# Prompt attention on one Trainium2 core: value tiles stationary, two query tiles moving

## What is computed

```python
# fox: causal, with a forgetting bias
s = q @ k.T * SCALE + (q_cum - k_cum);   p = softmax(where(k_pos <= q_pos, s));   o = p @ v
# nsa, selected branch (here all 16 blocks of 64 keys are selected, so it is causal over all keys)
s = q @ k_sel.T * SCALE + rel_bias;      p = softmax(causal);                      o_s = p @ v_sel
# nsa, window branch: the last 512 keys
s = q @ k_win.T * SCALE + rel_bias;      p = softmax(0 <= dist < 512);             o_w = p @ v_win
o = gate_c * o_c + gate_s * o_s + gate_w * o_w
```

## Time and profile before

| | |
|---|---|
| median of 3 runs | 2388.65 us (2384.7 to 2396.48) |
| profiled execution | 2383.58 us, its span 2381.8 us |
| busy: PE, PEld, DVE, ACT, POOL | 85%, 74%, 41%, 32%, 18% of the span |
| stage of `prompt_attention` | 874 to 1321 us |
| mean granted clock of TensorE | 0.91 of 2.4 GHz over the span, 0.97 in the stage |

### The profile page before, as it was taken

The page is one execution under the profiler, slowest core; times in us unless marked ns, Lnnn a source line. Parts: engine busy times, 40 slices in busy tenths (PEclk is TensorE's granted clock), DMA queues, the critical chain, the costliest instruction groups (busy, mean ns, idle before and its releaser), DMA issues. The chain is left out here.

```text
span 2381.8 us, 35846 instructions
## 1 busy us (share of the span) xinstructions
PE 2024.5 (85%) x12308; PEld 1761.7 (74%) x12308; DVE 979.1 (41%) x2016; ACT 771.3 (32%) x1469; POOL 431.5 (18%) x566
## 2 busy tenths in 40 slices
PE   3995979995637489999999488599999999799997
PEld 3884977785324489888988366599999999676764
DVE  2334223013223257676767521433333333355554
ACT  3223011112112126565656410322222222244454
POOL 4310002145061321121111000021212122000000
PEclk9896989997878559999999699699999999899998
DMA  5523635327683922232300041311111111402001
GB/s 128 96 66 105 206 143 185 116 72 196 217 266 125 169 62 54 54 79 55 68 16 1 31 140 69 110 44 45 44 44 53 35 53 35 150 32 71 26 27 47
DMA packets 164114, 210.37 MB, mean 88 GB/s; under 512 B 43420, under 2 KB 119509, under 8 KB 163863
## 3 DMA queue, kind: packets, MB, share of 16 engines
q1 hardware_dynamic: 136250, 125.09, 18.2%
q0 software_dynamic: 27744, 83.78, 12.6%
HBM read 173.84 MB, written 40.18 MB: 90 GB/s over the span
## 5 line engine op out<-in xcount | busy, mean ns | idle before, releaser
L118 PE MATMUL y_acc<-w_down_split_hi,act_split_hi 128*128 128x512 f32 (+1 forms) x396 | 164.6, 416 | 19.9 <-DVE act_split_lo L2623 17.9
L118 PE MATMUL gate_acc<-h_T_hi,w_gate_split_hi 128*128 128x352 f32 x528 | 172.6, 327 | 9.0 <-POOL w_gate_split_lo L2473 9.0
L120 PE MATMUL gate_acc<-h_T_hi,w_gate_split_lo 128*128 128x352 f32 x528 | 170.9, 324 | 0.0
L119 PE MATMUL gate_acc<-h_T_lo,w_gate_split_hi 128*128 128x352 f32 x528 | 170.6, 323 | 0.0
L118 PE MATMUL up_acc<-h_T_hi,w_up_split_hi 128*128 128x352 f32 x528 | 170.2, 322 | 0.0
L120 PE MATMUL up_acc<-h_T_hi,w_up_split_lo 128*128 128x352 f32 x528 | 169.3, 321 | 0.0
L119 PE MATMUL up_acc<-h_T_lo,w_up_split_hi 128*128 128x352 f32 x528 | 169.3, 321 | 0.0
L2171 ACT ACTIVATE pa_scores<-pa_scores,pa_neg_max 128x128 f32<-128x128 f32 (+1 forms) x192 | 144.1, 751 | 68.9 <-DVE pa_neg_max L2205 62.3
L2179 ACT ACTIVATE pa_probs_T_hi<-pa_t 128x512 fp32r<-128x512 f32 (+3 forms) x288 | 125.0, 469 | 106.6 <-PE pa_t L2133 105.2
L2234 DVE TENSOR_TENSOR pa_probs_T_lo<-pa_t,pa_probs_T_hi 128x512 fp32r<-128x512 f32 (+3 forms) x288 | 144.7, 530 | 32.8 <-ACT pa_probs_T_hi L2179 30.8
L119 PE MATMUL y_acc<-w_down_split_lo,act_split_hi 128*128 128x512 f32 (+1 forms) x396 | 157.5, 398 | 0.0
(11 more groups left out here) (409 smaller groups left out, 4939.0 us busy)
## 6 DMA issues: line engine op xcount, KB each, us to landing
fox_k_pages<-in_cache_fox_kv SPq DMA_DIRECT2D x64, 256.0 KB, 8.7
w_rows<-in_cache_fox_kv POOLq DMA_DIRECT2D x64, 256.0 KB, 6.5
w_gate<-in_w_gu SPq DMA_DIRECT2D x22, 512.0 KB, 3.9
w_up<-in_w_gu SPq DMA_DIRECT2D x22, 512.0 KB, 3.9
w_down_half<-in_w_down SPq DMA_DIRECT2D x22, 512.0 KB, 3.9
sel_pages<-in_cache_nsa_kv POOLq DMA_DIRECT2D x64, 128.0 KB, 7.6
pa_k_fox<-scratch_kf_d POOLq DMA_DIRECT2D x32, 256.0 KB
w_rows<-in_w_in SPq DMA_DIRECT2D x3, 2048.0 KB, 14.4
```

The source lines that it names most:

```text
L118: pe.matmul(out, a[0][at], b[0][bt], start=start, stop=False)
L119: pe.matmul(out, a[0][at], b[1][bt], start=False, stop=False)
L120: return pe.matmul(out, a[1][at], b[0][bt], start=False, stop=stop)
```

## The change

Units are taken in pairs (query tiles 2p and 2p + 1; NPR = 24 pairs in a turn of the loop). The value tile, its hi and lo halves side by side (128 columns), is now stationary, and the turned probabilities of both query tiles (256 columns) move. The result O is transposed: 128 rows (64 of the hi values, 64 of the lo) by 2 x 128 queries. ScalarE copies it to SBUF (`oT`), and `back(p)` makes two plain float32 products of it with `add_halves` (two 64x64 identities stacked), which turn it back and add the two halves. VectorE copies that to the job's output. Where a key tile counts for only one of the two query tiles, the slot of the other holds zeros, which POOL writes once. Key tiles are laid out in `pT` by slots, counted from the last one down. Beside this, constants that only the sample attention uses go into a table of their own (`c_smisc`), some tiles move to other phases or shrink, the ninth value tile goes away, and a local name in `down` changes.

```diff
+    NPR = NU // 2
+    def slots(s):
+        j, t = units[s]
+        out = []
+        for key in range(t, first_tile(s) - 1, -1):
+            r = t // 2 * 2 + 1 - key
+            out.append((key, NT if jobs[j][1] == "win" and t % 2 == 0 and r == 5 else r))
+        return out
+    def pair_slots(p):
+        seen = dict((slot, key) for s in (2 * p, 2 * p + 1) for key, slot in slots(s))
+        return sorted(seen.items())
...
-        scaled = ph.sb("pa_job_scaled", [P, NT, HD])
-        pT = [split(ph, f"pa_probs_T{i}", [P, T]) for i in range(2)]
+        pT = [split(ph, f"pa_probs_T{i}", [P, NT + 1, 2, P]) for i in range(2)]
+        oT = [ph.sb(f"pa_out_T{i}", [P, 2 * P]) for i in range(2)]
...
+            for both in pT:
+                for t in both:
+                    for slot, half in ((0, 0), (NT, 1)):
+                        pool.tensor_copy(t[:, slot, half, :], c.zero[:, :].to_broadcast([P, P])).then_inc(s_z, 1)
...
-            pe.wait_ge(pa.s_vz, 6)
+            pe.wait_ge(s_z, 12)
...
-                def values(s):
-                    pe.wait_ge(s_cd, i * NCK + of_unit[s][-1] + 1)
-                    pe.wait_ge(s_n, i * NU + max(0, s - 1) + 1)
-                    for x in range(m):
-                        at = first_tile(s) + x
+                def values(p):
+                    pe.wait_ge(s_cd, i * NCK + of_unit[2 * p + 1][-1] + 1)
+                    pe.wait_ge(s_n, i * NPR + max(1, p))
+                    mine = pair_slots(p)
+                    for x, (slot, key) in enumerate(mine):
                         for w_ in range(2):
-                            ins = pe.matmul(O[s % 2][:, 0:2 * P], pT[s % 2][w_][:, x * P:(x + 1) * P],
-                                            v[kind][u][:, at:at + 2, :, :].rearrange("p t w e -> p (t w e)"),
+                            ins = pe.matmul(O[p % 2][:, 0:2 * P], v[kind][u][:, key, :, :].rearrange("p w e -> p (w e)"),
+                                            pT[p % 2][w_][:, slot, :, :].rearrange("p a n -> p (a n)"),
...
+                def back(p):
+                    pe.wait_ge(s_ev, i * NPR + p + 1)
+                    for half in range(2):
+                        at = 2 * P + half * HD
+                        ins = pe.matmul(O[p % 2][:, at:at + HD], oT[p % 2][:, half * P:(half + 1) * P], misc(c, "add_halves", P),
+                                        start=True, stop=True)
+                    ins.then_inc(s_bk, 1)
-                for s in range(NU + 3):
+                for s in range(NU + 5):
                     if s < NU:
                         scores(s)
                     if 0 <= s - 2 < NU:
                         turn(s - 2)
-                    if 0 <= s - 3 < NU:
-                        values(s - 3)
+                    if s >= 6 and s % 2 == 0:
+                        back((s - 6) // 2)
+                    if s >= 4 and s % 2 == 0 and s - 3 < NU:
+                        values((s - 4) // 2)
...   (scalar)
+                    if s >= 5 and s % 2 == 1:
+                        p = (s - 5) // 2
+                        act.wait_ge(s_o, i * NPR + p + 2)
+                        act.wait_ge(s_bk, i * NPR + max(0, p - 1) + 1)
+                        act.activation(oT[p % 2][:, :], O[p % 2][:, 0:2 * P], ACT.Copy).then_inc(s_ev, 1)
...   (vector)
-                    dve.wait_ge(s_o, i * NU + s + 2)
-                    dve.tensor_reduce(oj[j % 2][:, t, :], O[s % 2][:, 0:2 * HD].rearrange("p (w e) -> p e w", w=2), AX, ALU.add).then_inc(s_n, 1)
+                    dve.wait_ge(s_bk, i * NPR + p + 2)
+                    dve.tensor_copy(oj[j % 2][:, t - 1:t + 1, :], O[p % 2][:, 2 * P:2 * P + 2 * HD].rearrange("p (t e) -> p t e", t=2)).then_inc(s_n, 1)
...
-                    if 0 <= s - 4 < NU:
-                        output(s - 4)
+                    if s >= 7 and s % 2 == 1:
+                        output((s - 7) // 2)
...   (front, sync)
             sp.dma_start(c.misc[:, :], d["c_misc"]).then_inc(s_ms, 16)
+            sp.dma_start(c.smisc[:, :], d["c_smisc"]).then_inc(s_ms, 16)
```

More of the change, by code:

```diff
@@ L1795, in compressed_attention @@
         pT = [ph.sb(f"ca_probs_T{i}", [NC, H, P]) for i in range(2)]
+        g_raw = [ph.sb(f"pa_group_v_raw{n}", [P, NT, HD]) for n in range(2)]
         mx = ph.sb("ca_max", [P, 2, H])
@@ L1816, in _ @@
         def _(pool):
[L1818 to L1821, removed]
             for u in range(2):
@@ L1993, in prompt_attention @@
         oj = [ph.sb(f"pa_job_out{i}", [P, NT, HD]) for i in range(2)]
-        scaled = ph.sb("pa_job_scaled", [P, NT, HD])
-        bias = {kind: [ph.sb(f"pa_bias_{kind}{i}", [P, T]) for i in range(2)] for kind in kinds}
+        width = {"fox": T, "sel": T, "win": WIN + P}
+        bias = {kind: [ph.sb(f"pa_bias_{kind}{i}", [P, width[kind]]) for i in range(2)] for kind in kinds}
         sc = [ph.sb(f"pa_scores{i}", [P, T]) for i in range(3)]
-        pT = [split(ph, f"pa_probs_T{i}", [P, T]) for i in range(2)]
+        pT = [split(ph, f"pa_probs_T{i}", [P, NT + 1, 2, P]) for i in range(2)]
+        oT = [ph.sb(f"pa_out_T{i}", [P, 2 * P]) for i in range(2)]
         nm = ph.sb("pa_neg_max", [P, NU])
@@ L2164, in _ @@
             with act.Fori(0, 4) as i:
-                for s in range(NU + 2):
+                for s in range(NU + 4):
                     if 0 <= s - 1 < NU:
@@ L2224, in output @@
                         ins.then_inc(s_co, 1)
-                for s in range(NU + 4):
+                for s in range(NU + 6):
                     if s < NU:
@@ L2580, in pair @@
                 half, grp = passes[q]
-                n = sum(ROWS[t] for t in tiles_of(grp))
+                n = sum(ROWS[t] for t in bothof(grp))
                 if grp == 0:
@@ L2692 @@
 MISC = {}
+SMISC = {}
 def constants():
@@ L2714, in constants @@
     c["c_one"] = np.eye(NBK + 1, dtype=np.float32)[:, NBK:]
-    parts = {}
+    parts, own = {}, {}
     w = np.arange(P)
@@ L2720, in constants @@
     seq, head, query = r // HQ, r % HQ // NQ, r % NQ
-    parts["wmask_s"] = np.where(w[None, :] <= query[:, None], np.float32(NEG), np.float32(0))
+    own["wmask_s"] = np.where(w[None, :] <= query[:, None], np.float32(NEG), np.float32(0))
     ms = np.zeros((P, NSEL), np.float32)
@@ L2737, in constants @@
     parts["seen"] = seen.reshape(P, NT * H)
-    parts["causal_new"] = np.where(np.arange(NQ)[None, :] > query[:, None], np.float32(NEG), np.float32(0))
+    own["causal_new"] = np.where(np.arange(NQ)[None, :] > query[:, None], np.float32(NEG), np.float32(0))
     spread = np.zeros((P, 2, P), np.float32)
@@ L2748, in constants @@
     c["c_misc"] = np.concatenate(list(parts.values()), axis=1).astype(np.float32)
+    at = 0
+    for k, v in own.items():
+        SMISC[k] = (at, at + v.shape[1])
+        at += v.shape[1]
+    c["c_smisc"] = np.concatenate(list(own.values()), axis=1).astype(np.float32)
     return c
```

135 lines of the change are left out of this document (73 added, 62 removed).

## The result

Both kernels were timed in seven executions each: before 2388.65 us (2384.7 to 2396.48), after 2402.66 us (2396.01 to 2411.13). The ratio is 1.0053, 95% interval 1.0031 to 1.0074: the change makes the kernel slower, by about 12.6 us. The profiled spans say the same, 2381.8 and 2394.1 us. The forecast was 2383, some 6 us faster; the time lies in the range (2345 to 2405) and on the other side of before.

What follows compares the result with a forecast made beforehand. TensorE seemed to bound the stage, but engine hand-overs decide: 2381.8 - 3 (turns) + 1 (start) = 2380 us of span; carrying over -2 us and taking -4 more gave a 2383 us median, range 2345 to 2405.

Steps and rivals of the forecast that it cites:

- TensorE's slots: In the changed stage, TensorE's work falls from 97 to 82 us a turn, 60 us over four turns if nothing else mattered.
- rivals 3 and 4: TensorE: clock falls to half, about 2700 us, chance 0.03; value products with stationary value tile cost above 0.119, no own chance.
- rival 1: TensorE's saved slots count in full because engines buffer better: up to 60 us, half of it giving 2358; chance 0.35.
- The price of the way back: Back's two plain f32 products on TensorE cost 0.25 us a pair, 6 us a turn, ends 0.13 and 0.44.
- rival 2: Way back dearer, 0.44 a pair plus waits for ScalarE's copy: 29 us over 96 pairs, 2412 us; chance 0.17.
- The walk of a sel job: Job's hand-overs between engines: PE waits for the low half in odd steps, leaving 0.4 us gain a job, 16.9 us after.
- The extra -4 us: First value product behind transposes takes 0.08 us extra, once a pair instead of twice: 8 us, half hidden by waits.
- The ends: At each turn's end the last pair's transposes, copies and back are uncovered, costing 1.4 us a turn.
- The start: At the stage's start PE newly waits for eight zero fills on POOL; about 1 us is left.
- Other stages: All stages of the kernel except the changed one were to stay within 1 us.

Runs made afterwards that it cites:

- the two experiments: The changed kernel with the way back in bf16, 2387.31 us; the changed kernel with each of the way back's two products issued twice, 2433.37 us.
- the split kernel: The changed kernel with half of a pair's value products in the even step, half in the odd, and back one step later: 2369.61 us, 0.992 of before.

## Why the prediction was wrong, point by point

- **TensorE's slots.** Right. The value products start 0.12 apart, PE's share fell from 95% to 85% (forecast about 80%, with a cheaper way back and a shorter stage), the clock of the stage stayed at its level (0.97 before, 0.96 after): rivals 3 and 4 are out, and rival 1, the full gain, too.
- **The price of the way back.** This is the step that failed first. I took the 32 records of line 1889 in the earlier trace rows for 32 products. They are sixteen (eight heads of two query tiles): a plain float32 product is two records, as the x4 of the two products of a pair in after shows. Sixteen in 7.09 us are 0.44 each at half clock, 0.22 at full, and two of them would have given 0.44 a pair. Measured: 0.37 where nothing waits, 0.38 as the median of after. I had 0.44 as an upper end and called it a half-clock price; it was nearly the price at full clock. The error is 0.13 x 96 = 12 us of slots, of which by the two experiments half to three quarters count, 6 to 9 us. That is rival 2 without its wait: in the prediction's sum the sign turned at 0.30 a pair, and the slot was above that. By the measured shares the price alone doesn't turn it, though: with 0.25 a pair, after would still be some 4 to 7 us slower than before (an estimate; no run has that price).
- **The walk of a sel job.** Its mechanism is right. Uneven steps make PE stand ahead of the transposes for the low half (with the wait at the value products 19.7 us before and 65.2 after; "from 20 us to 60 or more" was forecast), and a job stays long although TensorE has less to do: 17.4 to 18.1 us as against 17 to 17.5. Its size is off: instead of 0.4 us gained a job, 0.05 to 0.5 are lost. Beside the way back's price it lacks a rule, a term that the prediction put at nothing: value products of pair p wait for the output copy of pair p - 2. In the sel job of after the way back begins at 1070.64 and the value products only at 1071.36, 0.72 us later. Moving the copy brought 5 us. How large the walk's other errors are is not taken apart.
- **The extra -4 us** for the first value product behind transposes was an addition by hand to the walk. The slot did go away once a pair (one product at 0.2 us in a pair, behind the way back, where there were two behind transposes). But it is TensorE time of the kind that the walk mostly gives back, and nothing measured stood behind crediting half of it on top. No run measures it alone.
- **The ends.** Right in size: 1.4 us a turn was forecast, 6.7 us over four turns were measured, 1.7 each. The landmark was wrong. I expected the first scores of the next turn 13 us behind the last maximum; they come 9.5 us behind it (1099.81 to 1109.30). The gap that PE had in the earlier trace rows now stands on VectorE, whose last output is the late one, as its timeline shows:

```profile
1109.43 0.29 DVE L2257 COPY pa_job_out<-pa_o 128x128 f32<-128x128 f32 x1 [2.62 <-PE pa_o L2182]
...
1113.49 0.29 DVE L2247 CUSTOM_DVE_ANT_0 pa_scores<-pa_s,pa_bias_fox 128x128 f32<-128x128 f32 x1 [3.34 <-issue]
```

- **The start.** Right: 1 us forecast, 1.2 to 1.3 measured.
- **Other stages.** "Within 1 us" was wrong. POOL begins the stage at 873.83 before, at 877.71 in after and at 884.14 in the split kernel, behind stages that the kernels share, and what follows the stage takes 6.3 us less in after than before. Where these differences come from is open; the medians follow the stage's own lengths, within 7 us.

Together: 6 to 9 us from the way back, about 5 from the output copy's place, 1 to 2 from ends and start, and up to 4 from the -4 make 12 to 20 us; the forecast was 18 to 20 us off. These sizes come from different experiments, and that they add up so is not shown. What the runs do show is that, with the operands exchanged, the kernel is slower than before only with both: a way back in float32 that stands in the even steps and value products in those steps alone. With a way back in bf16, with the way back in the odd step, and with even steps it isn't slower.

## What to carry to other kernels

When one engine's work is nearly halved by batching two iterations, write down in which steps it falls. If it moves into every second step, the engines wait for each other in turns, and here that cost more (70 us) than the shorter list saved in that order (57); spread over both steps, the same instructions were 34 us faster, and 21 us faster than before. And price an instruction from a row of the same type by first counting how many records one instruction of the source leaves.

## What the runs showed of the hardware

- A plain float32 product of 128 stationary and 64 moving columns is two records and costs 0.18 to 0.19 us (after; the clock was 1.00 there); the same product in bf16 is one record and costs 0.03, a transpose of 128x128 float32 costs 0.07 to 0.11. The Trainium skill ("FP8 and Floating Point Precision", TensorE Precision Notes) says that true FP32 takes four passes through the array. By that, four times the bf16 product's 0.03, a product would cost 0.12 (an estimate). The trace has two records and 0.18 to 0.19, so here the measured price stands.
- TensorE work taken out of the way back was worth 15 of 31 us with uneven steps, 9 to 13 of 30 with even steps, and nothing of 22 with even steps and a longer VectorE instruction in its place.
